# A layer norm's column sums moved from GpSimd to TensorE, and its shift product moved one chunk forward

## The chip, the cores and the metric

The kernel runs on one core of one Trainium2 chip. The metric is the device time of one execution in microseconds (us), as the median of several runs. The core's engines are TensorE (PE in the profile; its weight loads are PEld), VectorE (DVE), ScalarE (ACT), GpSimd (POOL) and SyncE (SP, which here issues transfers).

## The reference, cut to what matters

One decoder layer runs over 272 prompt tokens and 32 sample tokens: an input projection, sparse attention and pooling, an output projection `w_out`, a layer norm, a gated MLP with a short convolution, and a second layer norm. The change touches the first of the two norms:

```python
mix = jnp.einsum('bqm,md->bqd', jnp.concatenate([a, m], axis=-1), w_out)
x = layer_norm(DEEPNORM_ALPHA * x + mix, ln1_g, ln1_b)
# layer_norm: mu = mean(x), var = mean((x - mu)^2) over the 2048 channels of a token
f, conv_state = conv_ffn(x, conv_prefix, w_up, conv_w, conv_b, w_down)
```

## The kernel before, in words

Channels lie on the 128 partitions and tokens on the free axis, so 2048 channels are 16 blocks of 128 x 290 (`NQ` = 290 tokens). A product is cut into slabs of 4 output blocks. A slab's accumulators are the four banks of the PSUM tensor `G`; a second PSUM tensor, `A`, has four banks for small products. Weights come in chunks of 512 KB (`raw`, a ring of 3). For chunk n, ScalarE rounds `raw` to `w_hi` (`hi(n)`, L1107), VectorE makes `w_lo = raw - w_hi` (`lo(n)`, L1460), and TensorE does 24 matmuls, three for each product of blocks (L486 to L488). `hi(n)` waits until TensorE is done with chunk n - 3, `chunk(n)` waits for `lo(n)`, and SyncE refills a slot of `raw` once `lo(n)` is done.

The stage around the change is the last part of the output projection: 4 slabs of 4 chunks, chunks `AO` to `AO + 15`, here called chunk 0 to chunk 15. They cover the attention's half of the channels; the pooling's half was added into `z1` before. Each engine goes through a list of its own in program order. The engines meet only at semaphores.

- TensorE: chunk by chunk. After chunk 5 comes the shift product (L924), one full-size matmul of ones with block 0, whose result is about each token's mean of block 0. It waits for the whole first slab. After chunk 15 come the norm's sums (L931 to L939).
- VectorE, at chunk f: `lo(f + 2)`, and then what the norm needs. `add_x` (L1890) adds the residual to a block, `unshift_partial` (L1885) and `unshift` (L1846) subtract the shift, four blocks at a time. At chunks 3, 7, 11 and 15 it adds the slab's four accumulators to `z1` (L1926), which sets `g_free`. The next slab's matmuls into a bank of `G` wait for this.
- ScalarE, at chunk f: `hi(f + 2)`, then `keep_shift` (L1344) at f = 5, which copies the shift out of PSUM, and `squares` (L1354), the squares of four blocks each, after the `hi` of f = 6, 9 and 13, and after the loop. There are four square buffers, so each group of squares waits until the one before it has been added up.
- GpSimd, `gather`: it adds blocks 0 to 11 into one sum (L1049) and their squares into another (L1053), 11 additions each, one after the other.
- `sums` then reduces over the partitions with matmuls whose stationary operand is a 128 x 32 block of ones. Quarter q of `A`'s partitions (32 rows) takes the q-th block of a group, so four such products go to four column groups of the array. The two gathered tiles take one such product each (L931, L932), blocks 12 to 15 four (L935), their squares four (L939). Each is in 32-bit floats and stands in the trace as two pieces.
- Then `totals` (L952 to L960), with some idle products (`warm`) between them, and the norm's scaling on VectorE, ScalarE and GpSimd, which feeds the next projection (`w_up`).

The second norm, at the end of the kernel, uses the same functions with `round_` = 1.

Of the kernel before, what the change touches and what calls it, by code (L numbers as in the profile page):

```python
# [10 lines left out]
T = TP + TS  # L11
# [18 lines left out]
KB = D // 128  # L30
# [8 lines left out]
MO, AO = 58, 74  # L39
# [5 lines left out]
SL_IQ, SL_Q, SL_K, SL_P, SL_V, SL_M, SL_A, SL_UP = 0, 1, 3, 4, 6, 7, 11, 15  # L45
SL_DN = SL_UP + NUP

M0 = META - 2
NQ = T - M0
# [18 lines left out]

CENTRE = (range(1, KB), tuple(k for k in range(1, KB) if k not in (2, 5, 8, 11, 14)))
GATHERED = 3 * 4 - 1  # L70


def slot_of(n):
# [24 lines left out]
def layer(nc, xT, w_iq, w_ik, w_in, w_out, w_up, w_down, kT_cache, v_cache, ik_cache, pages,  # L98
# [26 lines left out]
    ln_b = put("ln_b", [128, 9, NY], f32, xr)  # L125
# [97 lines left out]
    with ExitStack() as ctx:  # L223
# [259 lines left out]
        def _(pe):  # L483
# [436 lines left out]

            def shift_sum(z, last_slab, round_):

                pe.wait_ge(g_free, 4 * (last_slab + 1))
                pe.matmul(A[:, 0, 0:z.shape[2]], ones[:], z[:, 0, :], start=True, stop=True).then_inc(shift_mm, 1)  # L924

            def sums(z, tmp, slab, round_):

                n = z.shape[2]
                pe.wait_ge(z_gathered, GATHERED * (round_ + 1))
                pe.wait_ge(sq_gathered, GATHERED * (round_ + 1))  # L930
                pe.matmul(A[0:32, 1, 0:n], ones[:, 0:32], tmp[:, 1, :], start=True, stop=False)  # L931
                pe.matmul(A[32:64, 2, 0:n], ones[:, 0:32], tmp[:, 2, :], start=True, stop=False)  # L932
                for q in range(4):
                    pe.wait_ge(g_free, 4 * (slab + 3) + q + 1)
                    mm = pe.matmul(A[32 * q:32 * q + 32, 1, 0:n], ones[:, 0:32], z[:, 12 + q, :], start=q != 0, stop=True)  # L935
                mm.then_inc(part_mm, 1)
                for q in range(4):
                    pe.wait_ge(squared, KB * round_ + 12 + q + 1)
                    mm = pe.matmul(A[32 * q:32 * q + 32, 2, 0:n], ones[:, 0:32], tmp[:, 5 + q, :], start=q != 1, stop=True)  # L939
                mm.then_inc(part_mm, 1)  # L940
# [24 lines left out]
            for s in range(NOUT):  # L965
                for c in range(4):
                    chunk(AO + 4 * s + c, SL_A + s, CK * c, 0, 7, mix_parts, NQ)
                    if s == 1 and c == 1:
                        shift_sum(z1q, SL_A, 0)
            sums(z1q, ln_a, SL_A, 0)  # L970
            totals(ln_a, NQ, 0)
            warm(6)

# [26 lines left out]
        @block.gpsimd  # L1000
        def _(pool):
            PL = mybir.EngineType.Pool
            pool.memset(ones[:], 1.0).then_inc(preset, 1)
            pool.memset(tiny[:], EPS).then_inc(preset, 1)
            pool.memset(sc[:], NEG).then_inc(preset, 1)
            pool.memset(cand[:], 2.0).then_inc(preset, 1)
            pool.memset(tally[:].bitcast(f32), 0.0).then_inc(preset, 1)
            pool.memset(q_pad[:], 0.0).then_inc(preset, 1)
            pool.memset(p_score[:, 0:64], 0.0).then_inc(preset, 1)
            pool.wait_ge(pages_in, 16)  # L1010
            pool.wait_ge(x_high, 2)
            for g, b in [(0, b) for b in range(DB)] + [(1, 0)]:
                for j in range(2):
                    for i, r in enumerate(page_numbers(PL, NPG * b + 8 * j + 4 * g)):
                        pool.dma_start((ik_a, ik_b)[g][64 * j:64 * j + 64, b, i, :],  # L1015
                                       ik_cache[bass.ds(r, 1)].rearrange("a p n -> p (a n)")).then_inc(ik_in[2 * g], 16)
            pool.wait_ge(p_acc, IH)
            pool.wait_ge(preset, 7)
            for i, (t0, n, keys, col) in enumerate(PQ):
                view = p_score[0:n, col:col + keys]  # L1020
                pool.affine_select(out=view, in_=view, pattern=[[-1, keys]], compare_op=ALU.is_ge,
                                   fill=NEG if i else -FAR, base=t0, channel_multiplier=1).then_inc(p_causal, 1)

            pool.wait_ge(ctx_in, 16)
            pool.wait_ge(p_raw, IH)
            pool.wait_ge(iq_packed, 4)
            pool.memset(p_ext[:, :, 0:CTX], 0.0).then_inc(state_put, 1)
            pool.tensor_copy(p_ext[:, :, PS0:P_EXT].rearrange("p m (b w) -> p m b w", w=CTX + DQ)[:, :, :, 0:CTX],
                             p_state[:].rearrange("p m (b w) -> p m b w", w=CTX + DQ)[:, :, :, 0:CTX]).then_inc(state_put, 1)

            for u in range(1, 32, 2):
                load_value_unit(pool, PL, u)

            def centre(z, tmp, blocks, round_):

                pool.wait_ge(mean_kept, round_ + 1)
                for k in blocks:
                    pool.tensor_tensor(z[:, k], z[:, k], tmp[:, 0], ALU.subtract).then_inc(centred, 1)

            def gather(z, tmp, slab, round_):  # L1040

                for k in range(1, 12):
                    if k < 4:
                        pool.wait_ge(shifted, 4 * round_ + k + 1)
                    else:
                        pool.wait_ge(g_free, 4 * slab + k + 1)
                    if k > 1:
                        pool.wait_ge(z_gathered, GATHERED * round_ + k - 1)
                    pool.tensor_tensor(tmp[:, 1], z[:, 0] if k == 1 else tmp[:, 1], z[:, k], ALU.add).then_inc(z_gathered, 1)  # L1049
                    pool.wait_ge(squared, KB * round_ + k + 1)  # L1050
                    if k > 1:
                        pool.wait_ge(sq_gathered, GATHERED * round_ + k - 1)
                    pool.tensor_tensor(tmp[:, 2], tmp[:, 5] if k == 1 else tmp[:, 2], tmp[:, 5 + k % 4],  # L1053
                                       ALU.add).then_inc(sq_gathered, 1)

            gather(z1[:, :, M0:T], ln_a, SL_A, 0)
            centre(z1[:, :, M0:T], ln_a, CENTRE[0], 0)
            pool.wait_ge(x1_lo, KB)
            pool.wait_ge(rows_out, 32)
            pool.wait_ge(v_out, 16)  # L1060
            pool.wait_ge(p_out, 16)
            for i in range(NUP):

                for a in range(2):
                    if i:
                        pool.wait_ge(conv_v, i * 4)
                    pool.wait_ge(conv_in, 32)
                    src = c_state[:, 2 * i + FB * a:2 * i + FB * a + 2, 0:16].rearrange("p j (b w) -> p j b w", w=2)
                    dst = u_ext[:, 2 * a:2 * a + 2, PT:PT + 6 * DB].rearrange("p j (b w) -> p j b w", w=6)
                    pool.tensor_copy(dst[:, :, :, 0:2], src).then_inc(ctx_put, 1)  # L1070

                flat = c_state[:].rearrange("p j w -> p (j w)")
                for a in range(2):
                    pool.wait_ge(g_free, i * 4 + (4 * SL_UP + 2 * a + 2))
                    pool.wait_ge(ctx_put, i * 2 + 2)
                    dst = flat[:, i * 36 + 18 * FB * a:i * 36 + 18 * FB * a + 36].rearrange("p (j b w) -> p j b w", b=9, w=2)
                    src = u_ext[:, 2 * a:2 * a + 2, PT - 2:PT + 52].rearrange("p j (b w) -> p j b w", w=6)
                    pool.tensor_copy(dst, src[:, :, :, 0:2]).then_inc(tail_put, 1)  # L1078

            pool.wait_ge(h_split, 2 * NUP)  # L1080
            pool.wait_ge(tail_put, 2 * NUP)
            for k in range(KB):
                pool.tensor_tensor(z2[:, k], x_hi[:, k, META:T].bitcast(f32), x_lo[:, k, META:T].bitcast(f32),
                                   ALU.add).then_inc(residual, 1)
            gather(z2, ln_b, SL_DN, 1)
            centre(z2, ln_b, CENTRE[1], 1)


        @block.scalar
        def _(act):  # L1090
# [254 lines left out]

            def squares(z, tmp, g, slab, round_):
                if g:
                    act.wait_ge(sq_gathered, GATHERED * round_ + 4 * g - 1)
                for q in range(4):
                    if g == 0:  # L1350
                        act.wait_ge(shifted, 4 * round_ + q + 1)
# [4 lines left out]
            def norm(z, tmp, round_, split):  # L1356

                n = tmp.shape[2]
                par = (ln1_sb, ln2_sb)[round_]
                act.wait_ge(part_mm, 2 * round_ + 1)  # L1360
                act.activation(tmp[:, 3], A[:, 1, 0:n], ACT.Copy).then_inc(part_a, 1)
                act.wait_ge(var_done, round_ + 1)
                act.activation(ln_s[:, 3:6], ln_s[:, 0:3], ACT.Sqrt, bias=tiny[:, 15:16]).then_inc(sd_done, 1)
# [12 lines left out]
            z1q = z1[:, :, M0:T]  # L1376
            for f in range(AO, UP0):
                hi(f + 2)
                if f == AO + 5:
                    keep_shift(ln_a, 0)  # L1380
                if f in (AO + 6, AO + 9, AO + 13):
                    squares(z1q, ln_a, (f - AO - 5) // 4, SL_A, 0)
# [57 lines left out]
        def _(dve):  # L1440
# [406 lines left out]

            def norm(z, tmp, blocks, round_, split):
                n = tmp.shape[2]
                dve.wait_ge(part_mm, 2 * round_ + 2)  # L1850
                dve.tensor_copy(tmp[:, 4], A[:, 2, 0:n]).then_inc(part_b, 1)
                dve.wait_ge(total_mm, 2 * round_ + 1)
                then(dve.tensor_scalar(ln_s[:, 0:3], A[:, 0, 0:3], 1.0 / (32 * D), None, ALU.mult))
# [240 lines left out]
```

## Time and profile before

| | us |
|---|---|
| median of 3 runs | 1330.13 |
| lowest and highest | 1330.05, 1330.3 |
| the profiled execution's own time | 1327.27 |
| its span in the trace | 1325.6 |

The span runs from the first to the last record of the trace. The 1.7 us between it and the execution's own time lie around it. The profiled execution was 2.9 us faster than the median, so a sum made from the trace is a difference, which is then laid on the median.

### The profile page before, as it was taken

Reading aid. Unit: us, or ns where it says so; the run is one execution under the profiler, and the core shown is the slowest. Engines: PE = TensorE matmul, PEld = TensorE weight load, DVE = VectorE, ACT = ScalarE, POOL = GpSimd, SP = SyncE. Lnnn points to the kernel's source line nnn. Section 1 sums busy time; section 2 is a strip of 40 time slices with the busy share of each in tenths; the row PEclk is TensorE's granted clock in tenths of the full one; section 3 lists DMA queues with packets and bytes.
Section 4 is the critical chain, followed back from the end, with each engine's and each line's share of the span. In section 5 each row is a group of like instructions: output and inputs, shape, how many; then the busy total and the mean of one; then the engine's idle time right before and its main releaser. Section 6 shows DMA issues by size and latency. Waiting matters only on the chain.

```text
span 1325.6 us, 25349 instructions
## 1 busy us (share of the span) xinstructions
PE 1295.4 (98%) x9660; PEld 1210.2 (91%) x9660; DVE 775.1 (58%) x1263; ACT 597.8 (45%) x966; POOL 216.6 (16%) x325
## 2 busy tenths in 40 slices
PE   8999999999999899999999999999999999999995
PEld 8988777776679899999999999999999999999995
DVE  5657887674447685566556556556655545443444
ACT  4443322343333484554465455455545433333434
POOL 4510000023213530010001001000100500120202
PEclk9999999999999999999999999999999999999998
DMA  8868999989976365555555555555555655555552
GB/s 283 231 215 302 303 384 356 282 290 359 350 283 205 96 189 175 159 160 174 162 158 170 167 168 152 174 171 150 174 172 160 189 169 160 163 170 160 163 171 72
DMA packets 98988, 271.50 MB, mean 205 GB/s; under 512 B 13129, under 2 KB 21394, under 8 KB 98738
## 3 DMA queue, kind: packets, MB, share of 16 engines
q1 hardware_dynamic: 82978, 221.86, 53.7%
q10 hardware_dynamic: 8464, 28.88, 6.5%
q0 software_dynamic: 7424, 19.15, 4.2%
q8 instruction: 76, 1.25, 0.4%
q14 instruction: 46, 0.38, 0.1%
HBM read 264.66 MB, written 5.18 MB: 204 GB/s over the span
## 4 chain that ended last, share of the span: by engine, by line
PE 92%; DVE 4%; DMA 1%; issue 1%; ACT 1%; SPq 0%; DVEq 0%; ACTq 0%
PE G L486 28%; PE G L487 27%; PE G L488 27%; PE A L839 2%; PE A L654 2%; DMA k_ring<-in_kT_cache 1%; DVE w_lo L1460 1%; PE A L754 1%; PE A L670 0%; DVE z L1868 0%; DMA raw<-in_w_iq 0%; PE A L767 0%; DVE z L1885 0%; ACT w_hi L1107 0%; PE A L581 0%
## 5 line engine op out<-in xcount | busy, mean ns | idle before, releaser
L1460 DVE TENSOR_TENSOR w_lo<-raw,w_hi 128x1024 fp32r<-128x1024 f32 x353 | 436.2, 1236 | 395.9 <-ACT w_hi L1107 394.8
L1107 ACT ACTIVATE w_hi<-raw 128x1024 fp32r<-128x1024 f32 x353 | 372.8, 1056 | 502.1 <-PE G L488 453.4
L486 PE MATMUL G<-x_hi,w_hi 128*128 128x290 f32 (+1 forms) x1856 | 556.6, 300 | 4.6 <-DVE w_lo L1460 2.5
L487 PE MATMUL G<-x_lo,w_hi 128*128 128x290 f32 (+1 forms) x1856 | 551.1, 297 | 0.0
L488 PE MATMUL G<-x_hi,w_lo 128*128 128x290 f32 (+1 forms) x1856 | 547.9, 295 | 0.0
L486 PEld LDWEIGHTS G<-x_hi,w_hi 128*128 128x128 f32 x1856 | 348.3, 188 | 12.7 <-issue 11.5
L487 PEld LDWEIGHTS G<-x_lo,w_hi 128*128 128x128 f32 x1856 | 350.1, 189 | 0.2
L488 PEld LDWEIGHTS G<-x_hi,w_lo 128*128 128x128 f32 x1856 | 348.0, 188 | 0.0
L486 PE MATMUL G<-h_hi,w_hi 128*128 128x288 f32 x704 | 208.6, 296 | 0.0
L487 PE MATMUL G<-h_lo,w_hi 128*128 128x288 f32 x704 | 207.7, 295 | 0.0
L488 PE MATMUL G<-h_hi,w_lo 128*128 128x288 f32 x704 | 207.0, 294 | 0.0
L488 PEld LDWEIGHTS G<-h_hi,w_lo 128*128 128x128 f32 x704 | 132.6, 188 | 0.0
L487 PEld LDWEIGHTS G<-h_lo,w_hi 128*128 128x128 f32 x704 | 132.1, 188 | 0.1
L486 PEld LDWEIGHTS G<-h_hi,w_hi 128*128 128x128 f32 x704 | 131.9, 187 | 0.1
L1934 DVE SCALAR_TENSOR_TENSOR conv<-u_ext,cp_sb,conv 128x304 f32<-128x304 f32 x176 | 90.4, 534 | 44.1 <-ACT conv L1411 40.9
L1078 POOL COPY c_state<-u_ext 128x36 f32<-128x36 f32 x44 | 11.5, 262 | 368.9 <-ACT u_ext L1399 368.7
L1070 POOL COPY u_ext<-c_state 128x32 f32<-128x32 f32 x44 | 39.5, 928 | 132.8 <-DVE conv L1934 118.7
L1411 ACT ACTIVATE conv<-u_ext,cp_sb 128x304 f32<-128x304 f32 x88 | 51.5, 639 | 0.0
L486 PE MATMUL G<-a_hi,w_hi 128*128 128x290 f32 x128 | 39.1, 305 | 4.7 <-DVE z L1926 4.7
L1398 ACT ACTIVATE u_ext<-G 128x258 f32<-128x258 f32 x88 | 33.7, 383 | 16.9 <-PE G L488 14.3
L486 PE MATMUL G<-m_hi,w_hi 128*128 128x290 f32 x128 | 40.3, 315 | 0.0
L1015 POOL DMA_DIRECT2D ik_a<-in_ik_cache x64 | 33.3, 521 | 32.3 <-issue 29.3
(326 smaller groups left out, 1162.9 us busy)
## 6 DMA issues: line engine op xcount, KB each, us to landing
raw<-in_w_up SPq DMA_DIRECT2D x176, 512.0 KB, 3.6
raw<-in_w_down SPq DMA_DIRECT2D x88, 512.0 KB, 3.6
k_ring<-in_kT_cache SPq DMA_DIRECT2D x128, 256.0 KB, 4.9
raw<-in_w_in ACTq DMA_DIRECT2D x48, 512.0 KB, 5.5
raw<-in_w_out SPq DMA_DIRECT2D x32, 512.0 KB, 6.0
v_ring_x<-in_v_cache SPq DMA_DIRECT2D x32, 256.0 KB, 5.7
v_ring_x<-in_v_cache POOLq DMA_DIRECT2D x28, 256.0 KB, 6.2
v_ring_p<-in_v_cache SPq DMA_DIRECT2D x20, 256.0 KB, 5.4
```

What stands on the lines that cost most here:

```text
L486: pe.matmul(out, hi, xh, start=start, stop=False)
L487: pe.matmul(out, hi, xl, start=False, stop=False)
L488: return pe.matmul(out, lo, xh, start=False, stop=stop)
L654: mm = pe.matmul(A[32 * h:32 * h + 32, bank, :], q_pad[:, b, 2 * h:2 * h + 2, :], k_ring[:, slot:slot + UNIT, 128 * h:128 * h + 128], star ...
L839: mm = pe.matmul(A[32 * i:32 * i + 32, 2, :], p_tok[:, b // 4, b % 4, UNIT * u + i, :], value_slot(w, i), start=u == 0, stop=u == 3)
L1015: pool.dma_start((ik_a, ik_b)[g][64 * j:64 * j + 64, b, i, :], ik_cache[bass.ds(r, 1)].rearrange("a p n -> p (a n)")).then_inc(ik_in[2 * g ...
L1070: pool.tensor_copy(dst[:, :, :, 0:2], src).then_inc(ctx_put, 1)
L1107: act.activation(w_hi[:, c, 0:width], raw[:, c, 0:width], ACT.Copy).then_inc(hi_done, 1)
L1398: act.activation(u_ext[:, j, 0:PT], G[:, j, 0:PT], ACT.Copy).then_inc(act_own, 1)
L1411: act.activation(conv[:, j, 0:UO], u_ext[:, j, 0:UO], ACT.Identity, scale=cp_sb[:, t, 0:1], bias=cp_sb[:, t, 3:4]).then_inc(conv_a, 1)
L1460: dve.tensor_tensor(w_lo[:, c, 0:width], raw[:, c, 0:width], w_hi[:, c, 0:width].bitcast(f32), ALU.subtract).then_inc(lo_done, 1)
L1934: return dve.scalar_tensor_tensor(out=conv[:, j, 0:UO], in0=u_ext[:, j, w:w + UO], scalar=cp_sb[:, t, w:w + 1], in1=conv[:, j, 0:UO], op0= ...
```

## The change

- The shift product stands behind chunk 4 instead of chunk 5, and waits for block 0 alone. ScalarE's copy of it stands in turn 4 of its list instead of turn 5.
- GpSimd no longer gathers for the first norm. Its 22 additions go away.
- TensorE sums every group of four blocks and their squares itself, with eight products of the quarter form, accumulated in banks 1 and 2 of `A`: `first_sums(0)` behind chunk 8, `first_sums(1)` behind chunk 11, `first_sums(2)` behind chunk 14 and `first_sums(3)` behind chunk 15, the last in place of `sums`.
- ScalarE's squares of groups 1 to 3 wait for TensorE's sums of the group before, not for GpSimd's. The counts of `part_mm` are moved to match. The second norm keeps its gathering.

```diff
+SUMS = {(2, 0): 0, (2, 3): 1, (3, 2): 2}
             def shift_sum(z, last_slab, round_):
-                pe.wait_ge(g_free, 4 * (last_slab + 1))
+                pe.wait_ge(g_free, 4 * last_slab + 1)
                 pe.matmul(A[:, 0, 0:z.shape[2]], ones[:], z[:, 0, :], start=True, stop=True).then_inc(shift_mm, 1)
+            def first_sums(g):
+                if g == 0:
+                    pe.wait_ge(shifted, 4)
+                for q in range(4):
+                    if g:
+                        pe.wait_ge(g_free, 4 * (SL_A + g) + q + 1)
+                    mm = pe.matmul(A[32 * q:32 * q + 32, 1, 0:NQ], ones[:, 0:32], z1q[:, 4 * g + q, :], start=g == 0, stop=g == 3)
+                mm.then_inc(part_mm, 1)
+                for q in range(4):
+                    pe.wait_ge(squared, 4 * g + q + 1)
+                    mm = pe.matmul(A[32 * q:32 * q + 32, 2, 0:NQ], ones[:, 0:32], ln_a[:, 5 + q, :], start=g == 0, stop=g == 3)
+                mm.then_inc(part_mm, 1)
...
                     chunk(AO + 4 * s + c, SL_A + s, CK * c, 0, 7, mix_parts, NQ)
-                    if s == 1 and c == 1:
+                    if s == 1 and c == 0:
                         shift_sum(z1q, SL_A, 0)
-            sums(z1q, ln_a, SL_A, 0)
+                    if (s, c) in SUMS:
+                        first_sums(SUMS[s, c])
+            first_sums(3)
...
-            gather(z1[:, :, M0:T], ln_a, SL_A, 0)
             centre(z1[:, :, M0:T], ln_a, CENTRE[0], 0)
...
             def squares(z, tmp, g, slab, round_):
                 if g:
-                    act.wait_ge(sq_gathered, GATHERED * round_ + 4 * g - 1)
+                    if round_:
+                        act.wait_ge(sq_gathered, 4 * g - 1)
+                    else:
+                        act.wait_ge(part_mm, 2 * g)
...
-                if f == AO + 5:
+                if f == AO + 4:
                     keep_shift(ln_a, 0)
```

## Rows read from the trace of the kernel before

**Rows 1.** The page: the chain that ended last, shares of the span by engine.

```profile
PE 92%; DVE 4%; DMA 1%; issue 1%; ACT 1%; SPq 0%; DVEq 0%; ACTq 0%
```

**Rows 2.** Stretches: each engine's busy us and instructions, granted clock, DMA share, GB/s.

```profile
435.00:440.00 5.00, 2.31 (x10) 2.34 (x11) 5.00 (x10) 1.06 (x1) 0.81 (x1) 0.77 0.54 179
440.00:445.00 5.00, 5.00 (x35) 5.00 (x35) 2.41 (x5) 2.24 (x5) 0.77 (x1) 0.89 0.38 111
...
600.00:700.00 100.00, 100.00 (x752) 100.00 (x751) 58.39 (x74) 52.82 (x90) 9.56 (x16) 1.00 0.56 164
```

**Rows 3.** Waits of TensorE from 395 to 490 us: total, times, longest.

```profile
PE G L486 <- DVE z L1926: 4.7, 2, 2.7
```

**Rows 4.** TensorE's timeline at the ends of chunks 7 and 11.

```profile
419.68 0.29 PE L488 MATMUL G<-a_hi,w_lo 128*128 128x290 f32 x1
421.94 0.37 PE L486 MATMUL G<-a_hi,w_hi 128*128 128x290 f32 x1 [1.96 <-DVE z L1926]
...
434.68 0.29 PE L488 MATMUL G<-a_hi,w_lo 128*128 128x290 f32 x1
437.69 0.56 PE L486 MATMUL G<-a_hi,w_hi 128*128 128x290 f32 x1 [2.72 <-DVE z L1926]
```

**Rows 5.** TensorE's timeline around the shift product, and at the projection's end.

```profile
412.79 0.29 PE L488 MATMUL G<-a_hi,w_lo 128*128 128x290 f32 x1
...
413.54 0.30 PE L487 MATMUL G<-a_lo,w_hi 128*128 128x290 f32 x1
...
451.98 0.29 PE L488 MATMUL G<-a_hi,w_lo 128*128 128x290 f32 x1
```

**Rows 6.** VectorE's timeline from 414 to 438 us.

```profile
414.06 1.58 DVE L1885 TENSOR_TENSOR z<-z,ln_a 128x290 f32<-128x290 f32 x4 [1.76 <-ACT ln_a L1344]
...
416.69 1.57 DVE L1846 TENSOR_TENSOR z<-z,ln_a 128x290 f32<-128x290 f32 x4
419.72 1.70 DVE L1460 TENSOR_TENSOR w_lo<-raw,w_hi 128x1024 fp32r<-128x1024 f32 x1 [1.46 <-ACT w_hi L1107]
421.34 1.55 DVE L1926 TENSOR_TENSOR z<-G,z 128x290 f32<-128x290 f32 x4
...
427.76 3.93 DVE L1885 TENSOR_TENSOR z<-z,ln_a 128x290 f32<-128x290 f32 x4
...
437.10 1.55 DVE L1926 TENSOR_TENSOR z<-G,z 128x290 f32<-128x290 f32 x4
```

**Rows 7.** ScalarE's timeline: shift copy, squares of group 0, two roundings.

```profile
413.61 0.42 ACT L1344 ACTIVATE ln_a<-A 128x290 f32<-128x290 f32 x1 [2.57 <-PE A L924]
...
417.17 1.56 ACT L1354 ACTIVATE ln_a<-z 128x290 f32<-128x290 f32 x4 [2.20 <-DVE z L1846]
418.64 1.05 ACT L1107 ACTIVATE w_hi<-raw 128x1024 fp32r<-128x1024 f32 x1
...
435.07 1.06 ACT L1107 ACTIVATE w_hi<-raw 128x1024 fp32r<-128x1024 f32 x1 [2.14 <-PE G L488]
```

**Rows 8.** GpSimd's timeline: its first gathering addition, and its last.

```profile
417.60 1.33 POOL L1049 TENSOR_TENSOR ln_a<-z 128x290 f32<-128x290 f32 x1 [42.08 <-DVE z L1846]
...
450.33 1.83 POOL L1053 TENSOR_TENSOR ln_a<-ln_a 128x290 f32<-128x290 f32 x1
```

**Rows 9.** VectorE's groups by shape, 380 to 410 us: count, busy us, mean ns.

```profile
L1460 DVE TENSOR_TENSOR w_lo<-raw,w_hi 128x1024 fp32r<-128x1024 f32 x7 | 8.5, 1224 | 7.1 <-ACT w_hi L1107 7.1
```

**Rows 10.** The chain: the quarter-form sums after chunk 15, and a wider quarter product.

```profile
453.00 0.70 PE A L935 x8
453.69 0.69 PE A L939 x8
...
340.57 0.99 PE A L839 x8
```

**Rows 11.** TensorE's timeline: two matmuls of a chunk right behind quarter-form products.

```profile
386.91 0.40 PE L486 MATMUL G<-m_hi,w_hi 128*128 128x290 f32 x1
387.15 0.29 PE L487 MATMUL G<-m_lo,w_hi 128*128 128x290 f32 x1
```

More of the change, by code:

```diff
@@ L69 @@
 CENTRE = (range(1, KB), tuple(k for k in range(1, KB) if k not in (2, 5, 8, 11, 14)))
-GATHERED = 3 * 4 - 1
+SUMS = {(2, 0): 0, (2, 3): 1, (3, 2): 2}
+GATHERED = 11
 def slot_of(n):
@@ L921, in shift_sum @@
             def shift_sum(z, last_slab, round_):
-                pe.wait_ge(g_free, 4 * (last_slab + 1))
+                pe.wait_ge(g_free, 4 * last_slab + 1)
                 pe.matmul(A[:, 0, 0:z.shape[2]], ones[:], z[:, 0, :], start=True, stop=True).then_inc(shift_mm, 1)
+            def first_sums(g):
[10 more added lines that the diff above has]
+                mm.then_inc(part_mm, 1)
             def sums(z, tmp, slab, round_):
                 n = z.shape[2]
-                pe.wait_ge(z_gathered, GATHERED * (round_ + 1))
-                pe.wait_ge(sq_gathered, GATHERED * (round_ + 1))
+                pe.wait_ge(z_gathered, GATHERED)
+                pe.wait_ge(sq_gathered, GATHERED)
                 pe.matmul(A[0:32, 1, 0:n], ones[:, 0:32], tmp[:, 1, :], start=True, stop=False)
@@ L1038, in centre, with gather @@
                     pool.tensor_tensor(z[:, k], z[:, k], tmp[:, 0], ALU.subtract).then_inc(centred, 1)
-            def gather(z, tmp, slab, round_):
+            def gather(z, tmp):
                 for k in range(1, 12):
                     if k < 4:
-                        pool.wait_ge(shifted, 4 * round_ + k + 1)
+                        pool.wait_ge(shifted, 4 + k + 1)
                     else:
-                        pool.wait_ge(g_free, 4 * slab + k + 1)
+                        pool.wait_ge(g_free, 4 * SL_DN + k + 1)
                     if k > 1:
-                        pool.wait_ge(z_gathered, GATHERED * round_ + k - 1)
+                        pool.wait_ge(z_gathered, k - 1)
                     pool.tensor_tensor(tmp[:, 1], z[:, 0] if k == 1 else tmp[:, 1], z[:, k], ALU.add).then_inc(z_gathered, 1)
-                    pool.wait_ge(squared, KB * round_ + k + 1)
+                    pool.wait_ge(squared, KB + k + 1)
                     if k > 1:
-                        pool.wait_ge(sq_gathered, GATHERED * round_ + k - 1)
+                        pool.wait_ge(sq_gathered, k - 1)
                     pool.tensor_tensor(tmp[:, 2], tmp[:, 5] if k == 1 else tmp[:, 2], tmp[:, 5 + k % 4],
                                        ALU.add).then_inc(sq_gathered, 1)
-            gather(z1[:, :, M0:T], ln_a, SL_A, 0)
             centre(z1[:, :, M0:T], ln_a, CENTRE[0], 0)
@@ L1084, in _ @@
                                    ALU.add).then_inc(residual, 1)
-            gather(z2, ln_b, SL_DN, 1)
+            gather(z2, ln_b)
             centre(z2, ln_b, CENTRE[1], 1)
@@ L1359, in norm @@
                 par = (ln1_sb, ln2_sb)[round_]
-                act.wait_ge(part_mm, 2 * round_ + 1)
+                act.wait_ge(part_mm, 2 * round_ + 7)
                 act.activation(tmp[:, 3], A[:, 1, 0:n], ACT.Copy).then_inc(part_a, 1)
@@ L1849, in norm @@
                 n = tmp.shape[2]
-                dve.wait_ge(part_mm, 2 * round_ + 2)
+                dve.wait_ge(part_mm, 2 * round_ + 8)
                 dve.tensor_copy(tmp[:, 4], A[:, 2, 0:n]).then_inc(part_b, 1)
```

## The prediction

> **What bounds the kernel now.** I read the chain of work that ended last first. TensorE holds 92% of it [rows 1]. Then I read stretches. In the middle of the next projection TensorE starts 752 matmuls in 100 us, one every 0.133 us, at clock 1.00 [rows 2]. A chunk of 24 is 3.2 us, and a microsecond won before that point comes back at the end, since nothing there waits. So the question is how much earlier that projection starts.
>
> The list of waits gives what TensorE waits for around the change: the addition of the accumulators on VectorE, twice, 4.7 us in all [rows 3]. The timeline gives the places. Chunk 7's last matmul takes its turn at 419.68, so its slot ends at 419.81, and chunk 8 starts at 421.94: 2.13 us. Chunk 11's slot ends at 434.81 and chunk 12 starts at 437.69: 2.88 us [rows 4]. Behind the second gap the clock is lower, a mean of 0.77 over 435 to 440 and of 0.89 over 440 to 445 [rows 2]. As full is 2.4 GHz and the other level 1.2, that is 2.3 + 1.1 = 3.4 us at half rate. What it cost can be read from the chunks: the last slot ends at 451.98 + 0.13 = 452.11 [rows 5], three chunks of 3.2 before it is 442.51, so chunk 12 took 4.82 us, 1.62 more than 3.2. TensorE had stood for 2.88 us before this fall. The gap of 2.13 us was followed by none.
>
> Why is VectorE late? Its timeline beside GpSimd's tells. GpSimd gathers from 417.60 to 452.16 [rows 8]. In that time four shift subtractions of the same form take 3.93 us, where four took 1.58 before it began, and a `lo` takes 1.70 [rows 6] against a mean of 1.22 before [rows 9]. Between the accumulator additions at 421.34 and 437.10 [rows 6] VectorE does four `lo`, 12 block operations and the four additions. At undisturbed pace (1.14 us from a `lo` to what follows, 0.37 per block) this is 4 x 1.14 + 16 x 0.37 = 10.5 us, and it took 15.8.
>
> **The change, part by part.**
>
> *GpSimd's 22 additions go.* Nothing else on GpSimd waits behind them until the centring, which waits for the mean in either kernel. The gain is VectorE's pace, counted in the two gaps below.
>
> *The shift product moves one chunk ahead.* It costs TensorE the same. Between the matmuls at 412.79 and 413.54 there would be two slots, 0.27 us, without it, so it costs 0.75 - 0.27 = 0.48 us [rows 5]. The block that it waits for was added before 407.4, so it doesn't wait. Chunk 4 ends at 412.92 - 3.2 = 409.72, and the product at 410.20. ScalarE's copy follows 0.2 us later (as 413.61 follows 413.41 [rows 5, 7]) at 410.4, and puts the `hi` queued behind it, once at 409.98, to 410.7. From there I take start-to-start distances from the rows: `hi` to `lo` 1.08, `lo` to the next operation 1.14, four block operations 1.49. `lo` of chunk 7 is at 411.8, the four partial subtractions at 412.95. The `hi` of chunk 8 waits for chunk 5, whose end stays at 413.4, and starts 0.26 later (as 435.07 behind 434.81 [rows 4, 7]), at 413.7. Its `lo` is at 414.75, `unshift` at 415.9 (before: 416.69 [rows 6]). So only 0.8 us of the 3.2 is left here. The squares start 0.48 later at 416.4 (before: 417.17), and the `hi` behind them at 417.85 (before: 418.64 [rows 7]). The next `lo` is at 418.9 and undisturbed, 1.14 instead of 1.62, so the accumulator additions start at 420.05 instead of 421.34. Chunk 8 starts 0.60 behind that, at 420.65. **First gap: 0.84 instead of 2.13, a gain of 1.29.**
>
> *TensorE's own sums.* One call is 16 quarter-form pieces. The chain gives eight of them 0.70 us, and the next eight 0.69 [rows 10]. To this come the changes of form: behind such products the first two matmuls of a chunk start 0.24 apart instead of 0.13 [rows 11], and about as little at the front is not excluded. I take 1.4 + 0.1 = 1.5 us for a call. Three calls lie between chunks, all on TensorE's path. **A loss of 4.5.** From below the price is 1.3 us (the 0.64 from the first L935 to the first L939, twice), from above 2.1: eight pieces with 512 columns took 0.99 [rows 10], twice, and the 0.1. That is a loss of 3.9 to 6.3.
>
> The Trainium skill, "TensorE: Matmul & The Clock Gate", section "Measured speedup vs the span model", has four packed tiles cost a single matmul and some 4 ns for each further tile. The single product above cost 0.48 us and eight quarter pieces 0.70, so the rows don't bear it out; by it a call would be about 1.0 us and three a loss of 3.0.
>
> *Do these calls wait?* Everything on TensorE queues behind a wait in them. `first_sums(0)`, at about 423.9, needs squares that ScalarE ends at 417.9. ScalarE can start group 1's when that call ends, near 425.4, and needs 1.5 us. `first_sums(1)` comes at 435.0. Group 2's squares follow the `hi` of chunk 15, which waits for chunk 12 (at 439.7) and takes 1.05; they end near 442.4, and `first_sums(2)` comes at 446.1. The table load behind them keeps only the `hi` for the next projection waiting. So none waits, by 4 us or more.
>
> *The second gap.* VectorE, undisturbed and now short of work in every chunk (1.14 + 1.49 = 2.6 us in 3.2), is done with chunk 13's `lo` at 434.2, as `hi` of it waits for chunk 10 (431.8). It adds bank 0 of the third slab before chunk 11 has ended. Chunk 11 ends at 420.65 + 3.27 + 1.5 + 9.61 = 435.03, `first_sums(1)` takes the array to 436.53, and chunk 12 follows at once. **The gap of 2.88 is gone and with it the half rate, 1.62: a gain of 4.5.** Without this cover the call would have cost the 1.5 that is charged above.
>
> *The end.* Chunk 15 ends at 436.53 + 9.6 + 1.5 + 3.2 = 450.83, against 452.11, which is 1.28 earlier. Behind it the two products of the gathered tiles go (four pieces, some 0.35 us, and GpSimd's last addition ended at 452.16 only). But the last group's last block is ready 0.8 us after the chunk: its addition starts 0.22 behind the chunk and ends 0.6 later. Then ten pieces follow, near enough where they stood before, relative to the chunk. I take 0.2 us as gain.
>
> The sum: 1.29 - 4.5 + 2.88 + 1.62 + 0.2 = 1.5 us won. The profiled execution would take 1325.8 instead of 1327.27. Its span carries no part of its own in this, so the difference goes onto the median: 1330.13 - 1.5 = **1328.6 us**.
>
> **The rivals.**
>
> *Cheap sums (1327.1).* If a call costs 1.0 us, the loss is 3.0 instead of 4.5. For it: the array could take four such products at once. Against it: the 0.70 and 0.69 of the rows, in the same form. 10%.
>
> *VectorE stays late (1329.3).* If GpSimd was not what slowed VectorE, the first gap shrinks only by the 0.64 us of the earlier shift, to about 1.5. Chunk 11 then ends near 435.7, the sums go on to 437.2, and the additions, at 436.5, come in time for it. Chunk 12 starts at 437.2 at full rate. Chunk 15 ends at 437.2 + 9.6 + 1.5 + 3.2 = 451.5. With the 0.2 that is a gain of 0.8. So the sums in the second gap help even then. Against it: the stretched instructions stand only where GpSimd works. 12%.
>
> *The clock falls elsewhere (1330.2 to 1332, slower).* TensorE's quarter products do little for the array, and the norm's chain has idle places, the longest 1.2 us. If one half-rate stretch as in [rows 2] falls there, 1.6 us are lost and the gain is gone; two would be 3.2, and the kernel slower by 1.7. It decides when TensorE stands or half stands for over the 2.1 us that the clock has been seen to bear. Here the first gap and a call are parted by a full chunk, and the norm's own gaps are as before. 8%.
>
> *It does nothing (1330).* At the upper price, 2.05 a call, the gain is nil. This and the other sizes between 1.3 and 2.1 make the forecast's own range, 1327.9 to 1329.9.
>
> **How the numbers follow.** The forecast has 65%, the three rivals 10, 12 and 8, and 5 are left for what I don't see. A measurement here tells apart some 0.2%, 2.7 us. Faster by that means under 1327.5: all of the cheap sums, and a tenth of the forecast, where the first gap closes too (0.84 more): 0.18. Slower means over 1332.8: part of the clock's rival and of the unseen, 0.04. The rest, 0.78, is within. The range for 8 in 10 reaches from the cheap sums to the first of the clock's two prices, 1326.9 to 1330.5.
>
> **What would show it.** In the profile of the changed kernel: no additions of `ln_a` on GpSimd near 417 to 452; VectorE's `lo` at 1.2 us throughout; the shift copy near 410.4; the accumulator additions near 420.05 and a gap of 0.8 behind chunk 7; no wait at chunk 12 and clock 1.00 over 435 to 445; three groups of 16 quarter pieces, each moving the next chunk by 1.5; the norm's last sums some 1.5 earlier. Wrong would be: a wait inside a call for squares or blocks, a call over 2 us, VectorE's instructions still stretched, or a clock under 1 in the norm.

## The result and the profile after

| | before | after |
|---|---|---|
| median, us | 1330.36 (8 runs) | 1326.28 (8 runs) |
| lowest and highest, us | 1328.86, 1331.38 | 1325.49, 1331.4 |
| profiled execution and its span, us | 1327.27, 1325.6 | 1331.4, 1329.7 |

The ratio is 0.9973, 95% interval 0.9963 to 0.9983. The changed kernel is faster by some 4 us. The forecast of 1328.6 would be a ratio of 0.9989, and its range ended at 1326.9, so the measured 1326.28 lies below it.

The profiled execution of the changed kernel was the slowest of its eight, and that of the kernel before was faster than all eight timed ones. So the spans can't be compared. The stage can. In every trace of this case the time from the first matmul of the next projection to the end of the span is 865.1 us, to within 0.1 us in all 14 traces. Chunk 4 ended at 409.72 in one kernel and at 415.88 in the other, behind the same instructions. What the change touches lies between: from chunk 4's end to the next projection's first matmul. I call this the stage from here on. It took 460.49 - 409.72 = **50.77 us before and 464.58 - 415.88 = 48.70 after: 2.07 us won**, where 1.5 had been forecast.

TensorE's timeline after, at the shift product, at chunk 8's start and around the call behind chunk 11:

```profile
415.88 0.65 PE L925 MATMUL A<-z,ones 128*128 128x290 f32 x2
...
426.83 0.37 PE L487 MATMUL G<-a_hi,w_hi 128*128 128x290 f32 x1 [0.71 <-DVE z L1945]
...
440.98 0.29 PE L489 MATMUL G<-a_hi,w_lo 128*128 128x290 f32 x1
441.20 0.70 PE L934 MATMUL A<-z,ones 128*32 128x290 f32 x8
...
442.31 0.40 PE L487 MATMUL G<-a_hi,w_hi 128*128 128x290 f32 x1
442.55 0.30 PE L488 MATMUL G<-a_lo,w_hi 128*128 128x290 f32 x1
```

It answers to [rows 4] and [rows 5]. The gap ahead of chunk 8 is 426.83 - (415.88 + 0.49 + 9.6) = 0.86 us, where 2.13 stood. Chunk 12's second matmul would take its slot at 440.98 + 0.27 = 441.25 without a call and takes it at 442.55. So the call costs 1.30 us and nothing waits. The chain after shows what a call is made of:

```profile
430.27 0.62 PE A L934 x8
430.90 0.49 PE A L938 x8
431.39 0.33 PE G L487
```

Eight pieces on the way in take 0.62, the next eight 0.49, and the first matmul behind them 0.33 instead of 0.13. That is 1.31 us.

VectorE's timeline after, the lines that answer to [rows 6]:

```profile
425.09 1.23 DVE L1479 TENSOR_TENSOR w_lo<-raw,w_hi 128x1024 fp32r<-128x1024 f32 x1 [1.46 <-ACT w_hi L1123]
426.23 1.55 DVE L1945 TENSOR_TENSOR z<-G,z 128x290 f32<-128x290 f32 x4
...
432.60 1.57 DVE L1904 TENSOR_TENSOR z<-z,ln_a 128x290 f32<-128x290 f32 x4
...
440.40 1.55 DVE L1945 TENSOR_TENSOR z<-G,z 128x290 f32<-128x290 f32 x4
```

Nothing is stretched: four subtractions take 1.57 where they took 3.93, and the accumulators are being added while chunk 11 still runs. The stretches of the stage all have clock 1.00. This one holds chunk 12's start and answers to [rows 2]:

```profile
440.00:445.00 5.00, 5.00 (x46) 4.14 (x45) 4.50 (x10) 1.06 (x1) 0.00 (x0) 1.00 0.49 126
```

### The profile page after: what moved, and what is told of

It is laid out like the page before. It is cut to its first block, busy times and chain, and to the rows that moved or that the text cites. A ratio compares the mean times of both kernels' runs of the same rounds, so it can differ in the third digit from the quotient of the medians.

```text
span 1329.7 us, 25394 instructions
## 1 busy us (share of the span) xinstructions
PE 1300.9 (98%) x9704; PEld 1212.2 (91%) x9704; DVE 769.3 (58%) x1263; ACT 598.5 (45%) x966; POOL 191.7 (14%) x303
## 4 chain that ended last, share of the span: by engine, by line
PE 90%; DMA 3%; DVE 3%; SPq 1%; issue 1%; ACT 1%; ACTq 0%; DVEq 0%
PE G L487 27%; PE G L488 27%; PE G L489 26%; PE A L840 2%; DMA k_ring<-in_kT_cache 2%; PE A L655 1%; DVE w_lo L1479 1%; PE A L755 1%; SPq L315 1%; DMA raw<-in_w_out 1%; PE A L671 0%; DMA raw<-in_w_iq 0%; ACT w_hi L1123 0%; DVE z L1887 0%; PE A L768 0%
## 5 line engine op out<-in xcount | busy, mean ns | idle before, releaser
L1953 DVE SCALAR_TENSOR_TENSOR conv<-u_ext,cp_sb,conv 128x304 f32<-128x304 f32 x176 | 90.2, 533 | 44.7 <-ACT conv L1430 41.5
```

The costliest lines, as they stand in the source:

```text
L1953: return dve.scalar_tensor_tensor(out=conv[:, j, 0:UO], in0=u_ext[:, j, w:w + UO], scalar=cp_sb[:, t, w:w + 1], in1=conv[:, j, 0:UO], op0= ...
```

## The experiments

Two questions were open: what fills the stage's 2.07 us, and where the rest of the measured 4.1 us is. Each run was timed together with the kernel before on the same chip. Each execution also lists its mean granted clock. In the first trace of before TensorE has no work after 1312 us of its 1325.6, and the clock is at half, 1.2 GHz (0.50 over 1316 to 1320). So even an execution without any other half-rate stretch has a mean near 0.996 (shift_only, 0.996). One stretch of 3.4 us at half rate lowers the mean by 1.7 / 1326 = 0.0013.

**before_again and before_third.** Both are the kernel before, unchanged.

> The kernel before, unchanged, beside itself. Theory A (the stage explains about 2 us of the 4.1 that were won, and the rest is scatter of the part ahead of it): a ratio of 1.000 give or take 0.001, and in the trace the time from the start to chunk 4 of the stage differs from 406.5 us by some us, while the stage and what follows take the same 919 us. Theory B (something that the profiled executions did not show makes the kernel before slower within or behind the stage): the time from chunk 4 to the end comes out 2 us longer than in the first trace.

> The kernel before against itself once more. The second comparison of identical code gave 0.9986 with an interval that leaves 1 out. Theory (each set of executions carries an offset of its own, from the part ahead of the stage, as large as 0.001 to 0.0015): a ratio between 0.9985 and 1.0015, and 865.1 us behind the stage in the trace. Rival (the kernel under study is always timed 0.14% lower than the kernel before): 0.9986 again.

before_again: 0.9986 (0.9977 to 0.9996), which identical code should not give. before_third: 1.0005 (0.9995 to 1.0015). So identical code came out 0.0014 apart, about 2 us, in one of two comparisons, more than the interval allows, and this did not come back in the other. A set of executions can carry an offset of its own. The stage of before_third took 50.57 us, that of before_again 52.24. So theory A's "the same 919 us" was wrong: one and the same stage differs by 1.5 us. Its windows show why. The first lies behind the first gap, the second in chunk 12:

```profile
424.00:426.00 2.00, 2.00 (x10) 2.00 (x10) 2.00 (x3) 0.00 (x0) 2.00 (x2) 0.50 0.61 227
...
442.00:444.00 2.00, 2.00 (x10) 2.00 (x10) 1.88 (x5) 0.00 (x0) 0.00 (x0) 0.54 0.59 168
```

Here the clock fell behind both gaps. In the first trace of before it fell behind the second alone [rows 2]. The gaps are the same in both: 1.96 and 2.7 us of idle time ahead of chunks 8 and 12. Theory B was right in so far as this stage came out 1.5 us longer than in the first trace.

**after_again and after_third.** Both are the changed kernel, unchanged.

> The changed kernel, unchanged. Theory A: chunk 4 to the start of the next projection takes 52.0 us again (54.0 before), and the ratio lies between 0.9970 (as measured) and 0.9985 (2 us). Theory B: the ratio stays at 0.997 and the stage alone does not hold the 4 us.

> The changed kernel once more. By stage and clock (0.5 us of stage at full rate, 1.6 to 2.3 us of clock) it should be 2.1 to 2.8 us faster than the kernel before, beside its own twin of this call too; mean granted clock 0.9952 against 0.9938; the stage 48.7 us.

The ratios are 0.9974 (0.9963 to 0.9985) and 0.9984 (0.9976 to 0.9993), the stages 48.71 and 48.72 us, both as expected. In three traces the changed stage agrees to 0.02 us, where the old one took 50.57 to 52.24. The mean clock over the executions was 0.99513, 0.99527 and 0.99473 (8, 11 and 11 executions). For the kernel before it was 0.99353, 0.99383, 0.99358 and 0.99392 (34, 29, 26 and 13, on four chips). (The 11 and 12 executions of before_again and before_third gave 0.99391 and 0.99342.) Weighted, 0.99504 against 0.99368. The difference is 0.00136 x 1326 = 1.8 us, give or take 0.5 by the scatter of the single executions. None of the 125 executions of the kernel before has a mean clock above 0.995, and 12 of the 30 of the changed kernel have 0.996.

The changed kernel's clock is not full throughout either. Its three traces and before_again have a stretch of 3.4 us at half rate near 12 to 17 us, ahead of everything that the change touches. Here are 10 to 20 us in the first trace of before, then in the first of the changed kernel:

```profile
10.00:20.00 10.00, 8.29 (x62) 8.32 (x63) 6.58 (x7) 5.29 (x7) 5.99 (x12) 1.00 0.98 351
...
10.00:20.00 10.00, 8.04 (x49) 7.83 (x49) 6.03 (x7) 5.50 (x7) 4.80 (x9) 0.83 0.98 318
```

TensorE is idle for 1.6 to 2.5 us ahead of its matmul near 12 us in all 14 traces, and 7 of them have this stretch. The 1.8 us are the stage's only as far as it is equally frequent in both kernels, which no run shows.

**shift_only.** The first half of the change alone:

```diff
-                pe.wait_ge(g_free, 4 * (last_slab + 1))
+                pe.wait_ge(g_free, 4 * last_slab + 1)
...
-                    if s == 1 and c == 1:
+                    if s == 1 and c == 0:
                         shift_sum(z1q, SL_A, 0)
...
-                if f == AO + 5:
+                if f == AO + 4:
                     keep_shift(ln_a, 0)
```

> The kernel before with the shift product behind chunk 4 and waiting for block 0 alone; GpSimd still gathers. Theory (VectorE is late because GpSimd slows it): the accumulator additions behind chunk 7 start 0.6 us earlier, chunk 8 too, and the second gap stays, near 2.9 us, with its half rate: 0.6 to 0.8 us won, ratio 0.9995. Rival (VectorE is late because the shift comes late): both gaps shrink, the second below 1.5 us, 2 us or more won, ratio 0.9985.

Both gaps stay:

```profile
422.81 0.37 PE L486 MATMUL G<-a_hi,w_hi 128*128 128x290 f32 x1 [1.71 <-DVE z L1926]
...
438.53 0.37 PE L486 MATMUL G<-a_hi,w_hi 128*128 128x290 f32 x1 [2.67 <-DVE z L1926]
```

The first shrinks by 0.25 us only. GpSimd's additions start earlier too, and VectorE's `unshift` takes 2.19 us instead of 1.57, with 1.61 for the `lo` behind it (1.70 before), so the rest is lost again. In this execution the clock fell behind neither gap (1.00 over 417 to 446), and the stage took 48.94 us. That is 0.2 less than the 50.77 - 1.62 = 49.15 of before at full rate. So gaps of nearly the same length lead to a half rate or not: none, one or two such stretches stand in four traces with both gaps. The ratio was 0.9986 (0.9975 to 0.9996), equal to what the unchanged kernel gave beside it (before_again). Theory and rival both overrated the shift's place by itself; the rival's second gap below 1.5 us is refuted (2.67). The shift's place is worth 0.80 us with GpSimd silent (next run) and 0.2 beside it.

**sums_only.** The changed kernel with those three edits undone.

> The changed kernel with the shift product back behind chunk 5, waiting for the whole slab. Theory: the first gap is 1.6 to 1.7 us, 0.8 more than in the changed kernel, the second gap is gone, the clock stays full, and the stage takes 0.8 us more than in the changed kernel: 1.2 us won by the trace, ratio 0.999. Rival (the shift's place carries the gain): the second gap stays and the kernel is slower than before by the calls, 2 us or more, ratio 1.0015.

The stage took 49.50 us, 0.80 more than in the changed kernel, with a first gap of 1.48 us idle in place of 0.71, no second one, and clock 1.00. All as the theory had it. The ratio was 0.9976 (0.9967 to 0.9986), lower than the 0.999 expected; the offset of this set (0.9986 for the unchanged kernel beside it) is of that size.

**fill_gaps.** The kernel before, with idle products in the two gaps:

```diff
                     if s == 1 and c == 1:
                         shift_sum(z1q, SL_A, 0)
+                    for _ in range({(1, 3): 7, (2, 3): 10}.get((s, c), 0)):
+                        pe.matmul(A[:, 3, 0:128], ones[:], ones[:], start=True, stop=True)
```

> The kernel before with idle products of ones in both gaps (7 behind chunk 7, 10 behind chunk 11), nothing else changed; they reduce nothing and are read by no one. Theory C (most of what was won is the clock: the gaps let it fall, in the first gap in part of the executions, in the second in most): no half-rate stretch in the stage, which takes 49.2 us from chunk 4's end to the next projection instead of 50.8 or 52.2, a mean granted clock of all executions near 0.9953 instead of 0.9935, and 2 to 2.5 us won, ratio 0.998. Rival D (the won time is waiting, the clock is a minor part): at most 1.6 us won, in the executions that have the one half-rate stretch, and the mean clock rises by at most 0.0012.

VectorE is as late as before (chunk 12 starts 27.98 us behind chunk 4's end, 27.97 before), yet the stage takes 49.23 us at full rate, and the mean clock of its 11 executions is 0.99518. The ratio is 0.9988 (0.9979 to 0.9997): 1.6 us, with 2 to 2.5 inside the interval. The mean clock rose by 0.00135 above that of the kernel before beside it, give or take 0.0006. Rival D allowed 0.0012 and 1.6 us, so neither the clock nor the time refutes it. What the trace shows is that the half rate can be had back without any change to what VectorE does. In the stage that is 1.54 of the 2.07 us between the first two traces (50.77 - 49.23), and in measured time 1.6 us beside some 3.1 for the changed kernel.

**pool_busy.** The changed kernel, with GpSimd adding again, on tiles that nobody reads:

```diff
+            own = preset
+            pool.wait_ge(shifted, 1)
+            pool.memset(ln_a[:, 1:3], 0.0).then_inc(own, 1)
+            for k in range(1, 12):
...
+                pool.tensor_tensor(ln_a[:, 1], ln_a[:, 1], ln_a[:, 2], ALU.add).then_inc(own, 1)
+                pool.wait_ge(squared, k + 1)
+                pool.wait_ge(own, 7 + 2 * k)
+                pool.tensor_tensor(ln_a[:, 2], ln_a[:, 1], ln_a[:, 2], ALU.add).then_inc(own, 1)
```

> The changed kernel, in which GpSimd again does 22 additions of the same shape with the waits of its gathering, on two tiles of its own that nobody reads. Theory (GpSimd's reads slow VectorE): VectorE's instructions stretch again, a lo to 1.7 us and four block subtractions to over 2.5 us, the first gap grows to 1.3 to 1.5 us, the second stays covered by the call, and the stage takes 0.6 to 1 us more, 49.5. Rival (VectorE was late for another reason): VectorE's durations stay at 1.23 and 1.57, and the stage at 48.7.

VectorE's timeline:

```profile
421.78 1.23 DVE L1492 TENSOR_TENSOR w_lo<-raw,w_hi 128x1024 fp32r<-128x1024 f32 x1 [1.46 <-ACT w_hi L1136]
...
425.52 3.08 DVE L1922 SCALAR_TENSOR_TENSOR z<-x_b,z 128x290 f32<-128x290 f32 x4
...
429.66 3.58 DVE L1917 TENSOR_TENSOR z<-z,ln_a 128x290 f32<-128x290 f32 x4
433.16 1.72 DVE L1492 TENSOR_TENSOR w_lo<-raw,w_hi 128x1024 fp32r<-128x1024 f32 x1
```

The cause was right: the stretching is back, and GpSimd makes it. The consequence was wrong: the stage took 48.70 us, not a hundredth more. The `lo` ahead of the first gap was not hit this time (1.23), and the later delays end under the call behind chunk 11. So in this trace freeing VectorE of GpSimd wins nothing more. That is not general: in shift_only, with the shift product in the same place and the real gathering, the `lo` and the `unshift` ahead of it were hit, and the idle time ahead of chunk 8 was 1.71 us against 0.71. Ratio 0.9982 (0.9972 to 0.9992).

**calls_twice.** Eight more quarter products in each call, into an unused bank:

```diff
+                if g < 3:
+                    for _ in range(2):
+                        for q in range(4):
+                            pe.matmul(A[32 * q:32 * q + 32, 3, 0:NQ], ones[:, 0:32], z1q[:, 4 * g + q, :], start=True, stop=True)
```

> The changed kernel with eight more quarter-form products in each of the three calls between chunks, into an unused bank. Theory (the price is the pieces, 16 of them 1.3 us): the stage takes 3.7 to 3.9 us more, 52.5. Rival (four column groups run at once and the rest of a call is a fixed change of form): the eight products cost 1.0 us a call or less, 3 us or less in all.

```profile
426.12 0.62 PE A L934 x8
426.74 0.98 PE A L938 x16
427.72 0.49 PE A L942 x8
428.21 0.33 PE G L487
```

The stage took 51.54 us, 2.84 more, or 0.95 a call for eight products. The rival was right. Four quarter products, eight pieces, cost 0.49 us: what one full-size product of two pieces costs (0.48, worked out from [rows 5]). A call is 2 x 0.49 and a fixed 0.33 for the two changes of form. Ratio 1.0005 (0.9996 to 1.0015).

**no_sums.** The changed kernel without the first three groups' sums, so the norm's mean and variance come from the last four blocks alone, and it does not compute the reference. The sums behind chunk 15 start afresh (`start=True`, not shown). The calls are two products of 32 x 8 that carry the semaphore:

```diff
+                if g < 3:
+                    pe.wait_ge(squared, 4 * g + 4)
+                    for _ in range(2):
+                        pe.matmul(A[0:32, 3, 0:8], ones[:, 0:32], ones[:, 0:8], start=True, stop=True).then_inc(part_mm, 1)
+                    return
```

> The changed kernel without the sums of groups 0 to 2: each of the three calls between chunks is two products of 32 x 8 that carry its semaphore, so the norm's mean and variance are made from the last four blocks alone. GpSimd adds nothing either. Theory (with GpSimd silent VectorE is in time for chunk 12 without any cover, and the three calls are a pure price): no wait at chunk 12, clock full in the stage, and the stage takes 3.2 to 3.9 us less than in the changed kernel, 44.8 to 45.5 us. Rival (the call behind chunk 11 is what hides VectorE's lateness): a second gap of 0.5 us or more comes back, and the stage stays above 46.

```profile
435.11 0.22 PE A L934 x4
435.33 0.33 PE G L487
```

The stage took 45.98 us, with no wait at chunk 12 and clock 1.00. The number expected, 44.8 to 45.5, was missed, because the empty calls cost 0.42 us each by these rows (0.22 and 0.33 - 0.13). With them taken off, the stage would be 44.7, an estimate. The second gap that the rival wanted did not come back, though the stage lies only just under its 46: with GpSimd silent, VectorE is in time without cover. So by this estimate the three calls are a price of 4.0 us, paid to be rid of GpSimd's gathering. Ratio 0.9961 (0.995 to 0.9973).

**in_gap and in_gap_again.** The changed kernel with the first group's sums one chunk earlier, in the gap that is left:

```diff
-SUMS = {(2, 0): 0, (2, 3): 1, (3, 2): 2}
+SUMS = {(1, 3): 0, (2, 3): 1, (3, 2): 2}
```

> The changed kernel with the first group's sums behind chunk 7 instead of chunk 8. Its squares are ready 2 us before chunk 7 ends. Theory: the 1.4 us of the call cover the gap of 0.86 us that is left there, chunk 8 starts 1.4 us behind chunk 7, and the stage takes 47.8 us instead of 48.7; against the changed kernel 0.9 us won, against before 0.9965. Rival: the call delays VectorE's or ScalarE's work for chunk 9 and the 0.9 us come back as a wait: 48.7.

> The version with the first group's sums in the first gap once more: the stage 47.7 us, 1.0 less than the changed kernel of the same call, and its mean time 0.8 to 1.6 us below it.

In the chain the call takes 0.62 and 0.49 us again, and chunk 8 starts right behind it without a wait. The stages are 47.68 and 47.69 us, 1.0 less than the changed kernel's, where 0.9 had been expected. The ratios are 0.997 (0.9959 to 0.9982) and 0.997 (0.9959 to 0.998). Beside after_third, on the same chip, the second has a mean of 1325.48 against 1327.45. These 2.0 us are more than the 0.8 to 1.6 expected and than the 1.0 of the stage; the difference is of the size of the offset above. It is the fastest version here that computes the reference.

## Why the prediction was right in kind and wrong in size

With the terms of the sum put right, 2.25 us in place of 1.5 (below), the forecast would have been 1327.9, still inside its range. So two steps failed: the sum, above all the price of the calls, and the last one, "the difference goes onto the median". That one puts at nothing what a set of executions can differ by, where identical code later came out 0.0014 apart. The 1.8 us that lead out of the range lie there as far as is known; their cause is open.

- *The path and what is carried to the end.* Right: 865.1 us behind the stage in every trace.
- *The shift product and the first gap.* Right to 0.02 us. Counted from chunk 4's end, the shift copy starts at 0.69 (forecast 0.68), the squares at 6.67 (6.7), the accumulator additions at 10.35 (10.33), chunk 8 at 10.95 (10.93). The gap is 0.86 (0.84).
- *The calls, 4.5 us forecast.* **This is the term that was mis-sized.** They cost 1.39, 1.30 and 1.32, together 4.0, by the ends of the chunks, where 1.5 each was forecast. I had taken 0.70 and 0.69 for eight pieces from the chain at the norm's end [rows 10]. There the eight do not only run. The last pieces of L935 need the block whose addition VectorE begins at 452.51, and the last of L939 the squares that ScalarE ends at 453.65. Between chunks the same eight take 0.49. The other part of a call, 0.33 us, goes to the changes of form, for which I had taken 0.1. The rule of the Trainium skill that I had weighed and set aside ("TensorE: Matmul & The Clock Gate", "Measured speedup vs the span model") has four packed tiles cost a single matmul and some 4 ns for each further tile. calls_twice agrees with it: 0.49 us for four quarter products, 0.48 for one full-size product.
- *The second gap and its half rate, a gain of 4.5.* Right in the trace: 2.88 and 1.62 gone. **The half rate was slightly mis-sized over all executions.** I took it from the one profiled execution as a fixed 1.62. It came or not behind either gap, 1.8 us on average by the clocks, with the reservation made above. I had written that the clock bears a gap of 2.1 us; before_again shows that it need not. The times held a warning: the profiled execution was 2.9 us faster than the median, so it was no typical one.
- *The end, 0.2.* It was 0.32 from chunk 15's end at 456.52.
- *The waits inside a call.* None, as forecast. The third call's squares ended 3.8 us ahead of it (448.28 against 452.11). The forecast's own numbers, 442.4 and 446.1, made that 3.7, not its "4 us or more".
- *The sum.* 1.27 + 2.88 + 1.62 + 0.3 - 4.0 = 2.07 in the traces. At full rate alone it is 0.45, where the forecast's terms made it -0.13.
- *The rivals.* VectorE stays late: pool_busy made it so, and its reasoning (the calls cover it) was truer than its number, which was 0.7 us above the forecast where this trace shows no difference. The clock falling elsewhere: not behind chunk 4 in any of the eight traces with full calls; the half rate near 12 to 17 us stands in five of them, and in before_again too. Cheap sums: its 1327.1 lies nearest to the measured time, by luck, since a call cost 1.33 and not 1.0. Its reason, that four such products take the time of one, was right.

**The rest of the 4.1 us.** 0.45 from the stage at full rate and 1.8 from the clock are 2.25 us. The three comparisons of the changed kernel gave 0.9973, 0.9974 and 0.9984, on average 0.9977 or 3.1 us. The two of the unchanged kernel averaged 0.9995, or 0.6 us, so 2.4 are left between them. The first comparison's 4.1 us lie 1.8 us beyond the 2.25. An offset of nearly this size was seen with identical code (0.9986, 1.7 us between the medians), but nothing shows that the first comparison had one. So of the distance between 1.5 forecast and 4.1 measured, 0.6 us is the terms above in the traces, 0.2 the clock's average, and 1.8 is not accounted for by anything the change does in the stage. Its cause is open. The only stretch that varies in the traces, stage apart, is that ahead of chunk 4's end, 409.6 to 415.9 us. Part of this is the half rate near 12 to 17 us: the first matmul into `A` with x_hi (34 to 37 us) comes at 36.16 us on average in the seven traces that have it and at 34.60 in the seven that don't. Between the first two traces another 2.9 us arise from 119 to 249 us. No run took this stretch apart.

## What to carry to other kernels

Read the price of an instruction where nothing in its group waits for data: the same pieces cost 0.70 us at the norm's end, which held waits, and 0.49 between chunks. When TensorE stands for 2 to 3 us, ask of all executions and not of one trace whether the clock falls behind it. Small work that has to be done anyway belongs in such a gap: moved one chunk ahead, the first call took a gap of 0.86 us away and made the stage 1.0 us shorter. Time the unchanged kernel against itself before believing 0.1 or 0.2%.

## What the hardware showed that was not expected

- Nearly equal gaps, unequal clocks. Idle times of 1.7 to 2.7 us ahead of chunks 8 and 12 were followed by about 3.4 us at half rate in some executions and in others not: behind both in before_again, behind the second in two traces of before, behind neither in shift_only. Split by idle products down to 0.40 and 0.48 us, they were followed by none in the one trace of fill_gaps. An idle time of 1.6 to 2.5 us near 12 us was followed by such a stretch in 7 of 14 traces, after 1.75 us in no_sums and not after 2.45 us in before.
- Four products on four column groups of the array took the time of one, 0.49 us for eight pieces. To change from full-size matmuls to these and back cost 0.33 us, as much for 16 pieces as for 32.
- Beside GpSimd's additions four of VectorE's instructions with two operands in SBUF took as much as 3.93 us in place of 1.57 (before). The two engines need not touch the same tensor: in pool_busy GpSimd worked on `ln_a` alone, and the four of `z<-x_b,z` took 3.08.
